# Hybrid decoder layer on one core: the order of ScalarE's sums and copies in the forgetting stage, and the sample's own key product in four pieces

## The chip, the core and the metric

The kernel runs on one core of a Trainium2 chip. The metric is the device time of one execution in microseconds. Three runs of the kernel before gave 3106.99, 3108.30 and 3108.68 us, a median of 3108.3.

The engines are called as in the profile: PE is TensorE, PEld its weight loads, DVE VectorE, ACT ScalarE, POOL GpSimd, SP SyncE (here only the queue from which DMAs are issued). Each engine runs its own instructions in order; they wait for one another through semaphores.

## The reference, cut to what matters

One decoder layer runs for a prompt of 2048 tokens and a sample group of 8 sequences with one new token each. It has three mixers: dilated windows, forgetting attention and a state-space scan, then a gated feed-forward. The change lies in forgetting attention alone (4 heads of 64):

```python
# prompt: every query against all earlier keys
s = einsum('bqhe,bkhe->bhqk', qb, k) * SCALE
s = s + cq[..., :, None] - cum[:, :, None, :]      # cum: running sum of the log forget rates
s = where(causal, s, NEG_INF)
o = einsum('bhqk,bkhe->bqhe', softmax(s, axis=-1), vf)

# sample: one query against 4096 paged past keys and its own key
s_past = einsum('bthe,bshe->bhts', q, past_k) * SCALE + suffix + cn
s_new  = einsum('bthe,bshe->bhts', q, k) * SCALE   # the sample's own key
p = softmax(concatenate([s_past, s_new], axis=-1), axis=-1)
```

## The kernel before

`fox_stage` does forgetting attention. The prompt is cut into 16 blocks: 4 heads of 4 blocks of 512 queries, with 4, 8, 12 and 16 key tiles of 128 (the order of the sizes is turned round for odd heads). A step over one key tile is a slot; there are 160. Every engine walks the same slots in its own program, and the order within a slot is written out by hand.

For a block each score is computed twice. First comes `score` (L1033): 128 queries by up to 512 keys, in one of three banks of `s_ps`. DVE takes its row maximum (`maximum`, L869, reduction at L880), and ACT's `exp_sum` (L963, instruction L967) turns it into exponentials in place and adds them up; an accumulator read belongs to it. These sums are the denominators. `score` number u waits until the sum of number u - 3 is done, since it uses the same bank. They run one block ahead: during block b the scores of block b + 1 are done, and `scores_at` says which at which slot (one or two, or none). Second comes `score_turned` (L1055, L1069 to L1072) of the running block, keys by queries, with the block's maximum already inside; ACT's `exp` (L955, L961) writes the probabilities, and `value` (L1075, L1089) multiplies four tiles of them by V.

A part is a piece of 512 tokens of queries, keys or rates that is brought into place for later blocks. PE transposes it into the bank `z_ps` (`part`, L1015, transposes at L1028 and L1030). ACT's `high` (L933) copies it rounded to fp32r: for queries L939 and L940, for keys L945 and L946, for rates L948 alone. DVE's `low` (L854; L861 for queries, L865 for keys) waits for that copy and writes the rest of the value, so that two matmuls together keep the precision. `parts_at` (L461 to L465) says at which slot: there are 30 in the loop, and 29 of them fall on a slot that also has one or two scores. The bank z is also used by `turn_max` (L1100, L1104: the block's maxima as rows; ACT copies them at L953) and `turn_o` (L1093, L1097: the block's output turned back, which DVE scales at L905 and SP stores at L623). Each use waits for the one before it (`z_wait`, L1001).

Beside this the sample's decode runs, spread over the same slots by `Beside`. SP loads the pages (L615, 256 KB each) into a ring of 11 groups of four, POOL multiplies keys by the query (L678), DVE reduces (L709), and then, for each half of a sample's pages (16 halves, nine slots apart): PE turns the maxima (L821), DVE's `spread` (L720) takes the top (L722, L723), PE hands it to all partitions (L824), DVE subtracts (`shifted`, L729 to L733), ACT takes exponentials (L791, L792), PE multiplies by the page values (L804) and DVE's `keep` (L751, L757 to L768) adds the result to `o_heads`. L821 of one half waits until `keep` of the half before has read the bank (L763).

The sample's own key is handled once, in the opening. POOL multiplies `q_all` by `k_own` (L668, 8 samples of 256 columns) after its loads have landed. At slot 5 (`SET_UP`) DVE, behind its low half of that slot, adds `logf` to `rest` (L697), reduces the product per head (L702), scales it (L703) and sets `setup_done`. At slot 6 SP waits for that before it loads pages into the part of the ring that `k_own` occupied.

Order in a slot. PE: decode steps, scores, turned score, value, part, turn_o. DVE: decode steps, maxima, denominators, low half, normalise. ACT: decode exponentials, copy of the output, exp, high copies of the part, sums.

Of the kernel before, what the change touches and what calls it, by code (L numbers as in the profile page):

```python
# [16 lines left out]
ALU = mybir.AluOpType  # L17
ACT = mybir.ActivationFunctionType
AX = mybir.AxisListType
# [5 lines left out]
DEC = 8  # L25
# [5 lines left out]
HD = 64  # L31
# [403 lines left out]
def fox_stage(nc, area, load_next, inputs, pa, consts_d, gates, mb, kv_d, logf_s_d, logf_stored):  # L435
# [12 lines left out]
    GROUP, PROBS = 4, 6  # L448
    first_group = [f // GROUP for f in first]
    tiles_in = [[(j, k) for k in range(q + 1) for j in range(4)] for _, q in blocks]  # L450

    scores_at = {}
# [40 lines left out]
    def part_slot(a, step):  # L493
        return 5 + 9 * a + step

    with ExitStack() as ctx:
        def sb(name, shape, dt=F32):
            return ctx.enter_context(nc.sbuf_tensor(f"fp_{name}", shape, dt))
# [4 lines left out]
        def sem(name):  # L503
            return ctx.enter_context(nc.semaphore(f"fp_{name}"))
# [26 lines left out]
        s_own = sb("s_own", [P, DEC, H])  # L531
# [12 lines left out]
        k_own = spare[:, 4096:6144].rearrange("p (b f) -> p b f", b=DEC)  # L544
        q_all = spare[:, 6144:8192].rearrange("p (b f) -> p b f", b=DEC)
# [28 lines left out]
        own_mult, setup_done = sem("own_mult"), sem("setup_done")  # L574
# [6 lines left out]
        dve = Steps(sem("dve"))  # L581
# [3 lines left out]
        def quarter(n):  # L585
            at = n % RING
            ring, at = (kv_low, at) if at < RING - 4 else (kv_high, at - (RING - 4))
            return ring[:, at * QUART:(at + 1) * QUART]
# [76 lines left out]
        def decode_pool(pool):  # L665
            yield 2
            pool.wait_ge(own_landed, 16 * (4 + COLS))
            pool.tensor_tensor(k_own, q_all, k_own, ALU.mult).then_inc(own_mult, 1)  # L668

            def product(a, k):  # L670
                n = a * QUARTS + k
                pool.wait_ge(page_landed[n % RING], 16 * QUART * (n // RING + 1))
                if a % 2 == 0 and k == 0:
                    pool.wait_ge(q_in[a // 2 % 2], 16 * (a // 4 + 1))
                if n >= 2:
                    pool.wait_ge(reduced, n - 1)
                for pair in (slice(0, 2), slice(2, 4)):
                    last = pool.tensor_tensor(prod[:, n % 2, pair], quarter(n)[:, pair, 0],  # L678
                                              q_own[:, a // 2 % 2:a // 2 % 2 + 1].to_broadcast([P, 2, F]), ALU.mult)
                last.then_inc(multiplied, 1)  # L680

            for slot in range(part_slot(0, 0), part_slot(PARTS, 0)):
                yield slot
                for a in range(PARTS):
                    at = slot - part_slot(a, 0)
                    if at in range(0, 2 * QUARTS, 2):
                        product(a, at // 2)

        def decode_vector(v):
# [8 lines left out]
                                        rest[:].rearrange("p b h g -> p (b h) g"),  # L698
                                        logf[:].rearrange("p b h -> p (b h)").unsqueeze(2)
                                        .to_broadcast([P, DEC * H, PAGES]), ALU.add))  # L700
            v.wait_ge(own_mult, 1)
            dve.link(v, v.reduce_sum(s_own[:], k_own.rearrange("p b (h e) -> p b h e", e=HD), AX.X))  # L702
            dve.link(v, v.tensor_scalar(s_own[:], s_own[:], SCALE, None, ALU.mult))  # L703
            v.sem_inc(setup_done, 1)

# [144 lines left out]
        @block.vector  # L850
        def _(v):
            beside = Beside(decode_vector(v))

            def low(kind, *at):  # L854
# [75 lines left out]
        @block.scalar  # L930
        def _(act):
            beside = Beside(decode_scalar(act))

            def high(kind, *at):
                act.wait_ge(part_turned, part_no[kind, *at])
                z = z_ps
                if kind == "q":
                    r = at[0] % 3
                    act.activation(q_both[0:HD, r], z[0:HD], ACT.Copy, scale=SCALE)  # L939
                    last = act.activation(q_more[HD:P, r], z[0:HD], ACT.Copy, scale=SCALE)  # L940
                else:
                    x, cs = (at[0] % 2, slice(at[1] * QB, (at[1] + 1) * QB)) if kind == "k" else (
                        0, slice(at[0] * QB, (at[0] + 1) * QB))
                    if kind == "k":
                        act.activation(k_both[x][0:HD, cs], z[0:HD], ACT.Copy)  # L945
                        last = act.activation(k_both[x][HD:P, cs], z[0:HD], ACT.Copy)  # L946
                    else:
                        last = act.activation(k_more[x][0:AUGS, cs], z[0:AUGS], ACT.Copy)  # L948
                last.then_inc(part_hi, 1)

            def shift(b):
                act.wait_ge(m_turned, b + 1)
                act.activation(q_more[0:AUGS, b % 3], z_ps[0:AUGS], ACT.Copy).then_inc(m_rows, 1)  # L953

            def exp(b, i):  # L955
                u, q = first[b] + i, blocks[b][1]
                w = QB - max(0, i - 4 * q) * P
                act.wait_ge(turned, u + 1)
                if u >= PROBS:
                    act.wait_ge(valued, (u - PROBS) // GROUP + 1)  # L960
                act.activation(probs[:, u % PROBS, 0:w], t_ps[:, u % 2, 0:w], ACT.Exp).then_inc(exped, 1)  # L961

            def exp_sum(b, n):  # L963
                q, (j, k), u = blocks[b][1], tiles_in[b][n], first[b] + n
                s = s_ps[:, u % 3, 0:QB if k < q else (j + 1) * P]
                act.wait_ge(maxed, u + 1)
                act.activation(s, s, ACT.Exp, bias=neg[:, b % 2, j, k:k + 1],  # L967
                               accum_out=den[:, b % 2, j, k:k + 1]).then_inc(summed, 1)

            def exp_scale(b):  # L970
                at = scale[:, b % 2, :, 0:blocks[b][1] + 1]
                act.wait_ge(scale_in, b + 1)
                act.activation(at, at, ACT.Exp).then_inc(scale_ready, 1)

            def copy_o(b):
                act.wait_ge(valued, first_group[b + 1])
                if b:
                    act.wait_ge(o_turned, b)
                act.activation(oT[:], o_ps[:], ACT.Copy).then_inc(o_copied, 1)

            for b, (h, q) in enumerate(blocks):
                for i in range(size[b]):
                    beside.until(first[b] + i)
                    if i == 0 and b > 0:
                        copy_o(b - 1)
                    exp(b, i)
                    for part in parts_at.get((b, i), []):
                        high(*part)
                    for n in scores_at.get((b, i), []):
                        exp_sum(b + 1, n)  # L990
                if b + 1 < NBLK:
                    shift(b + 1)
                    exp_scale(b + 1)
            copy_o(NBLK - 1)
            beside.until(SLOTS + 100)
# [2855 lines left out]
```

## Time and profile before

| | us |
|---|---|
| median of 3 runs | 3108.3 |
| profiled execution | 3103.8 |
| its span | 3101.8 |
| granted clock, mean over the span | 0.976 |

| engine | busy in the span (3101.8 us) | busy in the forgetting stage (628 to 1018 us) |
|---|---|---|
| PE | 2931.8 | 328.4 |
| DVE | 1612.8 | 279.2 |
| ACT | 966.8 | 232.8 |
| POOL | 758.9 | 177.7 |

The profile's rows of groups give a line, an engine, an operation, the tiles written and read, the count, and then busy time, mean length, and idle time before with what ended it. A row of the timeline gives the start and the length in microseconds, then engine, line, operation and tiles; in brackets stands how long the engine had been idle before it and what ended that idle time. Tiles of the forgetting stage are called `fp_...`; `fp_store` holds the split queries and the keys of even heads, `fp_k_both` and `fp_k_more` the keys of odd heads.

### The profile page before, as it was taken

To read this page: it belongs to the slowest core of one execution; us is meant where nothing else is said; L and a number is where in the kernel's file an instruction comes from. 1 tells how busy PE (TensorE), PEld (TensorE's weight loads), DVE (VectorE), ACT (ScalarE), POOL (GpSimd) and SP (SyncE) were. 2 spreads that over 40 slices of the span, in tenths; PEclk is the share of its full clock that TensorE was granted. 3 is DMA by queue.
4 is the path that set the end of the run, shared out by engine and by line. 5 is a ranking of instruction groups with operands and counts; after the bars stand their busy time and mean duration, and the time that the engine had idled before them with its cause. 6 is when DMAs were issued, how large, how long until landed. Compare 5 with 4: busy or idle time off the path is not lost. (4 is left out here: it accounts for less than half of the span.)

```text
span 3101.8 us, 44538 instructions
## 1 busy us (share of the span) xinstructions
PE 2931.8 (95%) x15777; PEld 2466.8 (80%) x15777; DVE 1612.8 (52%) x3068; ACT 966.8 (31%) x2010; POOL 758.9 (24%) x570
## 2 busy tenths in 40 slices
PE   8999999978889899879979999999999999999998
PEld 5888889945445799768779999999997788888886
DVE  5122321257777688757655554455557444444445
ACT  4222322256566455533331211222213111111112
POOL 4001200035445354422202211112222111122210
PEclk9999999989999999989989999999999999999999
DMA  4554443476865343367551111111113411111101
GB/s 140 187 211 164 135 138 113 140 210 201 225 189 179 120 126 96 74 196 222 205 205 41 41 41 53 70 41 41 41 55 123 150 41 41 41 50 59 54 14 56
DMA packets 238390, 350.85 MB, mean 113 GB/s; under 512 B 75449, under 2 KB 173274, under 8 KB 232271
## 3 DMA queue, kind: packets, MB, share of 16 engines
q1 hardware_dynamic: 237303, 326.45, 33.6%
q0 software_dynamic: 944, 22.61, 2.0%
q8 instruction: 75, 1.23, 0.2%
q14 instruction: 68, 0.56, 0.1%
HBM read 284.19 MB, written 93.97 MB: 122 GB/s over the span
## 5 line engine op out<-in xcount | busy, mean ns | idle before, releaser
L2862 POOL TENSOR_TENSOR cm_dn_lo<-cm_dn_raw,cm_dn_hi 128x1024 fp32r<-128x1024 f32 x44 | 108.3, 2483 | 974.3 <-ACT cm_dn_hi L2911 974.3
L3152 PE MATMUL cm_g_ps<-cm_h_hi,cm_up_hi 128*128 128x344 f32 (+1 forms) x880 | 310.4, 353 | 11.1 <-DVE cm_h_lo L2967 10.9
L3154 PE MATMUL cm_g_ps<-cm_h_hi,cm_up_lo 128*128 128x344 f32 (+1 forms) x880 | 308.8, 351 | 0.0
L3152 PE MATMUL cm_u_ps<-cm_h_hi,cm_up_hi 128*128 128x344 f32 (+1 forms) x880 | 308.2, 350 | 0.0
L3153 PE MATMUL cm_g_ps<-cm_h_lo,cm_up_hi 128*128 128x344 f32 (+1 forms) x880 | 308.1, 350 | 0.0
L3154 PE MATMUL cm_u_ps<-cm_h_hi,cm_up_lo 128*128 128x344 f32 (+1 forms) x880 | 307.8, 350 | 0.0
L3153 PE MATMUL cm_u_ps<-cm_h_lo,cm_up_hi 128*128 128x344 f32 (+1 forms) x880 | 307.0, 349 | 0.0
L2855 POOL TENSOR_TENSOR cm_up_lo<-area,cm_up_hi 128x2048 fp32r<-128x2048 f32 x42 | 195.4, 4654 | 176.7 <-ACT cm_up_hi L2887 176.7
L2990 DVE TENSOR_SCALAR area<-area 128x344 f32<-128x344 f32 (+2 forms) x110 | 54.2, 493 | 330.4 <-ACT area L2904 189.6
L2900 ACT ACTIVATE area<-cm_g_ps 128x344 f32<-128x344 f32 (+1 forms) x110 | 55.0, 511 | 510.1 <-PE cm_g_ps L3154 509.9
L3152 PEld LDWEIGHTS cm_g_ps<-cm_h_hi,cm_up_hi 128*128 128x128 f32 x880 | 166.2, 189 | 36.3 <-issue 21.2
L3439 ACT ACTIVATE area<-pj_acc,area 128x480 f32<-128x480 f32 (+7 forms) x119 | 76.2, 641 | 345.8 <-PE pj_acc L3661 268.4
L3154 PEld LDWEIGHTS cm_g_ps<-cm_h_hi,cm_up_lo 128*128 128x128 f32 x880 | 166.4, 189 | 15.8
L3153 PEld LDWEIGHTS cm_g_ps<-cm_h_lo,cm_up_hi 128*128 128x128 f32 x880 | 166.3, 189 | 15.9
L3154 PEld LDWEIGHTS cm_u_ps<-cm_h_hi,cm_up_lo 128*128 128x128 f32 x880 | 165.4, 188 | 16.0
L3153 PEld LDWEIGHTS cm_u_ps<-cm_h_lo,cm_up_hi 128*128 128x128 f32 x880 | 165.3, 188 | 15.9
L3152 PEld LDWEIGHTS cm_u_ps<-cm_h_hi,cm_up_hi 128*128 128x128 f32 x880 | 165.2, 188 | 15.3
L3046 DVE TENSOR_TENSOR cm_y<-cm_y,cm_y_ps 128x1024 f32<-128x1024 f32 x88 | 107.4, 1221 | 122.8 <-PE cm_y_ps L3193 122.8
L2887 ACT ACTIVATE cm_up_hi<-area 128x2048 fp32r<-128x2048 f32 x44 | 84.3, 1917 | 278.6 <-PE cm_u_ps L3154 272.4
L3659 PE MATMUL pj_acc<-fp_store,pj_h_hi 128*128 128x480 f32 (+3 forms) x448 | 169.2, 378 | 0.9 <-DVE pj_h_lo L3508 0.9
L3660 PE MATMUL pj_acc<-fp_store,pj_h_hi 128*128 128x480 f32 (+3 forms) x448 | 167.8, 375 | 0.0
L3661 PE MATMUL pj_acc<-fp_store,pj_h_lo 128*128 128x480 f32 (+3 forms) x448 | 167.7, 374 | 0.0
(518 smaller groups left out, 7092.8 us busy)
## 6 DMA issues: line engine op xcount, KB each, us to landing
area<-in_w_up SPq DMA_DIRECT2D x44, 1024.0 KB, 7.0
fp_kv_low<-in_fox_kv SPq DMA_DIRECT2D x168, 256.0 KB, 3.0
area<-in_fox_kv SPq DMA_DIRECT2D x88, 256.0 KB, 2.9
cm_dn_raw<-in_w_down SPq DMA_DIRECT2D x44, 512.0 KB, 3.7
out_s_win<-in_cache POOLq DMA_DIRECT2D x8, 2047.0 KB, 8.3
area<-in_w_a SPq DMA_DIRECT2D x12, 960.0 KB, 7.9
proj_a<-area SPq DMA_DIRECT2D x48, 240.0 KB
sp_raw<-proj_b SPq DMA_DIRECT2D x16, 640.0 KB, 4.0
```

Source lines behind the costliest of these rows:

```text
L2855: pool.tensor_tensor(up_lo[:, s], up_raw[:, s], up_hi[:, s].bitcast(F32), ALU.subtract).then_inc(up_ready, 1)
L2862: pool.tensor_tensor(dn_lo[:, s], dn_raw[:, s], dn_hi[:, s].bitcast(F32), ALU.subtract).then_inc(dn_ready, 1)
L2887: act.activation(up_hi[:, s], up_raw[:, s], ACT.Copy).then_inc(up_hi_ready, 1)
L2900: act.activation(gate[:, s, HALO + at[b]:HALO + at[b + 1]], g_ps[:, b, 0:H.widths[b]], ACT.Copy).then_inc(gate_ready, 1)
L3046: v.tensor_tensor(y[:, n], y[:, n], sums(H, n).rearrange("p a n -> p (a n)"), ALU.add).then_inc(added, 1)
L3152: pe.matmul(out, hi, h_hi[:, k, cs], start=(k == 0), stop=False)
L3153: pe.matmul(out, hi, h_lo[:, k, cs], start=False, stop=False)
L3154: last = pe.matmul(out, lo, h_hi[:, k, cs], start=False, stop=(k == KT - 1))
L3439: act.activation(row[0:m, n % ROWS, 0:wide], acc[0:m, n % BANKS, 0:wide], ACT.Copy, scale=rstd[0:m, t:t + 1]).then_inc(evac, 1)
L3659: pe.matmul(out, h_hi[:, k, place(t)], w_hi[j % 2][:, k, 0:wide], start=(k == 0), stop=False)
L3660: pe.matmul(out, h_hi[:, k, place(t)], w_lo[j % 2][:, k, 0:wide], start=False, stop=False)
L3661: last = pe.matmul(out, h_lo[:, k, place(t)], w_hi[j % 2][:, k, 0:wide], start=False, stop=(k == KT - 1))
```

## The change

In `decode_pool` the one product over 8 samples becomes four over 2 samples each, each with its own step of `own_mult`. In `decode_vector` the one reduction over 8 samples becomes four, each waiting for its piece of the product. In ScalarE's loop over the slots, the loop over the slot's sums (`exp_sum`) and that over its parts (`high`) change places.

```diff
@@ decode_pool
             pool.wait_ge(own_landed, 16 * (4 + COLS))
-            pool.tensor_tensor(k_own, q_all, k_own, ALU.mult).then_inc(own_mult, 1)
+            for pair in range(0, DEC, 2):
+                two = slice(pair, pair + 2)
+                pool.tensor_tensor(k_own[:, two], q_all[:, two], k_own[:, two], ALU.mult).then_inc(own_mult, 1)
@@ decode_vector
-            v.wait_ge(own_mult, 1)
-            dve.link(v, v.reduce_sum(s_own[:], k_own.rearrange("p b (h e) -> p b h e", e=HD), AX.X))
+            for pair in range(0, DEC, 2):
+                two = slice(pair, pair + 2)
+                v.wait_ge(own_mult, pair // 2 + 1)
+                dve.link(v, v.reduce_sum(s_own[:, two], k_own[:, two].rearrange("p b (h e) -> p b h e", e=HD), AX.X))
             dve.link(v, v.tensor_scalar(s_own[:], s_own[:], SCALE, None, ALU.mult))
@@ scalar, the loop over a block's slots
                     exp(b, i)
+                    for n in scores_at.get((b, i), []):
+                        exp_sum(b + 1, n)
                     for part in parts_at.get((b, i), []):
                         high(*part)
-                    for n in scores_at.get((b, i), []):
-                        exp_sum(b + 1, n)
```

## Rows read from the trace of the kernel before

**Rows 1.** The page: busy time, share of the span and instructions of each engine.
```profile
PE 2931.8 (95%) x15777; PEld 2466.8 (80%) x15777; DVE 1612.8 (52%) x3068; ACT 966.8 (31%) x2010; POOL 758.9 (24%) x570
```

**Rows 2.** Table of stretches: stretch, length, busy time by engine, clock, DMA share, GB/s.
```profile
628.00:1018.00 390.00, 328.37 (x1968) 193.94 (x1968) 279.22 (x582) 232.79 (x608) 177.69 (x145) 0.93 0.69 199
```

**Rows 3.** Waits, 628 to 1018 us: who waited for whom, total, times, longest.
```profile
ACT fp_s L967 <- DVE fp_neg L880: 56.3, 46, 4.8
...
PE fp_s L1049 <- ACT fp_s L967: 21.1, 22, 2.5
...
DVE fp_k_more L865 <- ACT fp_k_both L946: 17.4, 7, 5.4
```

**Rows 4.** Lines L821 (first two rows) and L824: what ended their engine's idle time.
```profile
  DVE fp_o_heads L763: 9.3, 6
  DVE fp_o_part L763: 7.0, 6
...
  DVE fp_diag L723: 12.1, 11
```

**Rows 5.** Single lines: count, then shortest/median/longest in ns, first and last start.
```profile
L967 ACT ACTIVATE fp_s<-fp_s,fp_neg x156: 319/654/668, 631.7 to 1005.2; 128x512 f32<-128x512 f32 x111, 128x128 f32<-128x128 f32 x15, 128x256 f32<-128x256 f32 x15, 128x384 f32<-128x384 f32 x15
L967 ACT ACTIVATION_READ_ACCUMULATOR fp_s<-fp_s,fp_neg x156: 185/202/217, 632.2 to 1005.7; 128x1 f32 x156
...
L709 DVE TENSOR_REDUCE fp_s_dec<-fp_prod x64: 1201/1212/1223, 657.8 to 997.0; 128x16 f32<-128x1024 f32 x64
...
L678 POOL TENSOR_TENSOR fp_prod<-fp_kv_low,fp_q_own x84: 1254/1276/1459, 644.7 to 984.3; 128x512 f32<-128x512 f32 x84
```

**Rows 6.** Timelines of the opening: SP's queue, POOL, DVE and PE, 628 to 700 us.
```profile
634.52 31.06 SPq L615 DMA_DIRECT2D fp_kv_low<-in_fox_kv  x28
...
669.02 18.23 SPq L615 DMA_DIRECT2D area<-in_fox_kv  x16
687.29 0.43 SPq L623 DMA_DIRECT2D mix_b<-fp_o_tok  x1
...
639.00 4.52 POOL L668 TENSOR_TENSOR area<-area 128x2048 f32<-128x2048 f32 x1 [9.01 <-DMA fp_logf<-out_s_logf]
...
642.08 1.48 DVE L886 CAST fp_m_tok<-fp_top 128x4 fp32r<-128x4 f32 x1
...
653.02 2.29 DVE L702 TENSOR_REDUCE fp_s_own<-area 128x32 f32<-128x2048 f32 x1
...
690.48 0.42 DVE L905 TENSOR_TENSOR fp_o_tok<-fp_z,fp_rden 128x256 f32<-128x256 f32 x1 [5.68 <-DMA mix_b<-fp_o_tok]
...
693.19 1.03 PE L1030 MATMUL fp_z<-sp_consts,fp_k_tok 128*64 128x128 f32 x4 [3.83 <-DMA fp_k_tok<-proj_a]
```

**Rows 7.** Timelines of DVE and PE around slot 41.
```profile
751.07 0.68 DVE L880 TENSOR_REDUCE fp_neg<-fp_s 128x1 f32<-128x512 f32 x1
...
752.54 0.68 DVE L861 SCALAR_TENSOR_TENSOR fp_store<-fp_z,fp_store 64x512 fp32r<-64x512 f32 x1
...
753.83 0.27 PE L821 MATMUL fp_e<-sp_consts,fp_top_dec 128*4 128x128 f32 x1 [2.35 <-DVE fp_o_heads L763]
```

**Rows 8.** Timelines of ACT and PE around slot 105.
```profile
916.62 0.66 ACT L967 ACTIVATE fp_s<-fp_s,fp_neg 128x512 f32<-128x512 f32 x1 [0.64 <-DVE fp_neg L880]
...
917.86 1.10 PE L1097 MATMUL fp_z<-fp_fold,fp_oT 128*128 128x64 f32 x8 [0.68 <-DVE fp_store L861]
```

**Rows 9.** Timelines of DVE and PE behind slot 85.
```profile
858.85 0.68 DVE L861 SCALAR_TENSOR_TENSOR fp_store<-fp_z,fp_store 64x512 fp32r<-64x512 f32 x1 [0.95 <-ACT fp_store L940]
...
859.56 0.50 PE L1049 MATMUL fp_s<-fp_store 128*128 128x512 f32 x1 [1.62 <-ACT fp_s L967]
...
864.32 0.27 PE L821 MATMUL fp_e<-sp_consts,fp_top_dec 128*4 128x128 f32 x1 [1.83 <-DVE fp_o_part L763]
```

**Rows 10.** Timelines of ACT and PE around slot 97.
```profile
894.97 0.59 ACT L945 ACTIVATE fp_k_both<-fp_z 64x512 fp32r<-64x512 f32 x1 [1.83 <-PE fp_z L1030]
...
896.98 0.50 PE L1049 MATMUL fp_s<-fp_store 128*128 128x512 f32 x1 [1.58 <-ACT fp_s L967]
```

## The prediction

> **What bounds the kernel now.** I read five views in this order. The page's busy shares name TensorE (95%) [rows 1], but a share over the span says nothing of one stage, and the edit touches only the forgetting stage. Its window, 628 to 1018 us, is next [rows 2]: PE is busy 328 of 390 us, DVE 279, ACT 233. So PE has some 62 us of holes there, and anything that opens or closes a hole on PE moves the end, since every later stage starts after this one.
>
> The waits of the stage [rows 3] name two sorts of hole. The first is what the edit aims at: a prompt score (L1049) waits for ACT's sum (L967) of the tile three scores earlier, 21.1 us seen on PE. The same waits show ACT's sum waiting 56.3 us for DVE's maximum, so ACT isn't simply late; DVE often is. Third, DVE itself stands 17.4 us in front of the low half of a key part (L865) until ACT's high copy (L946) is done. DVE runs in order, so whatever stands behind that low half stands too.
>
> The second sort of hole is at the sample's decode steps [rows 4]: PE waits for DVE at L821 (until `keep` has read the output bank, 9.3 + 7.0 us in 12 times) and at L824 (until `spread`, 12.1 us in 11 times). These 28.4 us say that DVE is the later of the two engines at nearly every decode step. This decides the case: what makes DVE's low half later makes the next L821 or L824 later, and PE with it.
>
> **Part 1, ScalarE's order.** At 29 of the 160 slots there is both a part and a score to sum (12 slots with two sums, 17 with one). Before, ACT does: exp, high copies, sum(s). After: exp, sum(s), high copies. No instruction is added. PE and DVE keep their order: PE does scores, turned score, value, part transposes; DVE does maxima, then the low half. A sum costs 0.66 + 0.20 for its accumulator read [rows 5], less about 0.1 in which the two overlap: 0.75 us. The two copies cost 1.2 us (0.59 each, as the first of them in [rows 10]).
>
> So a sum ends up to 1.2 us earlier and the copies start up to 0.75 us (one sum) or 1.5 us (two) later. Queued behind the late copy: on ACT the next slot's exp; on DVE the low half, and behind it the reductions of the sample's products, the decode steps and the next maxima; on PE the next user of bank z (turn_o, turn_max or the next part). The part is free of delay only where the sums fit into time in which ACT waits for PE's transposes anyway. I walked the slots in the timeline, giving each engine its order and the durations it has there:
>
> Opening, slots 0 to 13. Earlier sums gain 0.7 us of PE at slot 0 and 1.3 us by slot 2; the late low half of slot 3 leaves 0.4 of that. Slot 5 (two sums) makes DVE 1.5 us later, slot 13 again 1.5. With 0.4 us of part 2 that is 1.5 + 1.5 + 0.4 - 0.4 = 3.0 us late at 687 us. None of this reaches the end, because a chain with no arithmetic in it ends last here [rows 6]: SyncE issues 28 page loads without a gap from 634.52 on, 16 more from 669.02, only then the store of the first output (687.29) and the next keys. DVE's L905 waits 5.68 us for that store, and PE's first part of head 1 waits 3.83 us for the keys. Neither the gate on the setup (L644, reached at about 668 us, opened at 655.5) nor those loads hang on the moved work. 3.0 is under 3.83: the opening costs nothing, with 0.8 us to spare.
>
> From 693 us on nothing covers. The slots, by kind:
> - Parts that come after a `value` (slots 29, 61, 73, 89): ACT waits 1 to 3 us for the transposes with the maxima long there, so the sums go into that wait. Copy and low half stay where they were, and the next waits of PE are on DVE: 0.
> - Slots 17 to 21: the same at first, PE gets its score 1.0 us earlier, and later copies give it back: -0.2.
> - One sum, maximum ready, copy late by one sum (slots 25, 63, 121, 137): L824, turn_max and L821 follow directly or through instructions without a gap. 0.8 + 0.75 + 0.75 + 0.8 = 3.1.
> - One sum whose maximum isn't ready, so that the copies wait for the maximum too. Slot 41 [rows 7]: the maximum ends at 751.75, the sum takes until 752.5, the copies until 753.7, so the low half starts at 753.75 instead of 752.54; behind it L763, and L821 on PE, which already waited 2.35 us for it: +1.2. Slot 105 [rows 8]: the sum starts at 916.62 as before, its 0.75 and the copies' 1.2 last until 918.57, the low half (0.68 [rows 7]) until 919.3, and turn_o, which had waited 0.68 us for it and started at 917.86, starts at about 919.35: +1.5. By the same working slots 57, 69 and 77 give 0.7 each (there DVE had other work before the low half). Together 1.2 + 1.5 + 2.1 = 4.8.
> - Two sums: slot 85 [rows 9]. The score after it waited 1.62 us for its sum and now doesn't; but the low half, which waited 0.95 us for the copy, moves 1.5 us, and so do the reductions and L763 behind it; at L821 PE had to wait 1.83 us and now waits for what it gained and 1.5 more: +1.5. Slot 81 is alike, with some 0.8 us covered by a store that L905 waits for at 850.49 (a second wait of the kind of L905 in [rows 6]): +0.7. Slot 93: DVE had 1.0 us of rest behind it: +0.5. Together 2.7.
> - Slots 97 to 101 [rows 10]: the sums of 97 fit into the 1.83 us before the copy, the score behind gains 1.58; then copy and low half of slot 99 are 0.55 late, those of 101 1.45, and turn_max 1.1. +1.1.
>
> Sum: 0 - 0.2 + 3.1 + 4.8 + 2.7 + 1.1 = 11.5 us. Three terms (63, 93 and 97 to 101, 2.35 us) I read through more than one wait, where part can be lost in others' slack; I count them at half: **+10.3 us**.
>
> **Part 2, the product in four pieces.** POOL's 4.52 us [rows 6] become four of the size of a page product, 1.28 us each [rows 5]: 5.1 us, ending at 644.1, before the first page product starts (644.71, which waited for its DMA). On DVE one reduction of 2048 columns takes 2.29 [rows 6] and one of 1024 takes 1.21 [rows 5], so 1.05 ns a column and 0.14 us fixed: four of 512 take 2.7 us, +0.4; three more links to itself cost between 0 and 0.1 us each. Nothing is gained by overlap: DVE comes to it at 653.0, POOL was done at 643.5. All four waits are met. Both additions lie in the opening, under the same loads: 0. If the cover is gone, it is 0.4 to 0.7 us. One side effect in the cover: the cast L886 at 642.08 [rows 6] took 1.48 us and ended with POOL's product; pieces could let it go earlier by up to 1.4 us. I take 0 for the whole, with +0.7 and nothing below it for the range, as 690.48 is set by the store.
>
> The Trainium skill (Perfetto Trace Analysis, Optimizing Scalar/DVE Operations) says that where these engines aren't saturated but cause bubbles elsewhere, breaking up instructions may let work complete sooner. By that rule both parts would pay; the trace agrees on the bubbles but not, for the pieces, on work that could start sooner. What it would give is rival A.
>
> **Rivals.**
> A, faster: the freed sums are what PE gets. The score waits right after the changed slots from 693 us on are 0.37, 0.72, 1.79, 1.62, 1.58 and 0.71 us, six of one pattern of which 1.62 and 1.58 stand in [rows 9, 10]: 6.8 us. If the late low halves are taken up by DVE's rests, the end is 6.8 us earlier. Place: DVE between the low half and the next L821 or L824; it decides where DVE rests there for longer than the copy is late (0.75 to 1.5 us). For it: 21.1 us of such waits. Against it: [rows 4]. 3101.5.
> B, no change: only the delays handed over directly count (25, 41, 69, 77, 105: 0.8 + 1.2 + 0.7 + 0.7 + 1.5 = 4.9), the others drown, or half of A comes off the forecast (10.3 - 6.8 = 3.5). 3111.8 to 3113.2.
> C, slower still: the cover of the opening fails, because the pieces or slot 13 cost over 0.8 us more than I think; up to 3.0 comes on top of 11.5: 3122.8.
> D, the order isn't what matters (ACT stands at the maximum whichever way): 0, part of B.
>
> **How the numbers follow.** The profiled execution took 3103.8 us (span 3101.8), 4.5 under the median of 3108.3. The working gives 3103.8 + 10.3 = 3114.1 for such an execution, and on the scale of the median 3108.3 + 10.3 = 3118.6. A measurement of this kernel can tell about 0.2% (6.2 us) from no change. Chances: forecast 0.57, C 0.11, B with D 0.20, A 0.12. The range takes in the forecast, B and most of C and leaves out A and the far end: 3104 to 3124. Slower 0.68, within 0.2% 0.20, faster 0.12.
>
> **What would show it.** Right: L967's releases of L1049 fall by 5 us or more after 693 us, while PE's waits for DVE at L821, L824, L1097 and L1104 and DVE's wait for L940/L946 grow by more; the low half of slot 41 starts 1.2 us later after its maximum; L905 still waits for a store and L1030 for the keys near 690 us, each about 3 us less; the stage ends 10 us later and later stages keep their length. Wrong: PE's waits at L821 and L824 don't grow (A), or head 1's first part no longer waits for a DMA (C).

## The result and the profile after

The changed kernel took 3126.9 us (median of 6 runs) against 3106.2 us before (6 runs): a ratio of 1.0069, 95% interval [1.0053, 1.0086], so 16 to 27 us slower. The forecast was slower by 10.3 us, 3118.6, with 3104 to 3124 as its range. The direction was right, the size was half of what came.

| | before | after |
|---|---|---|
| profiled execution, us | 3103.8 | 3119.8 |
| span, us | 3101.8 | 3117.8 |
| granted clock over the span | 0.976 | 0.973 |
| forgetting stage, first POOL memset to last normalise, us | 389.9 | 409.1 |
| DVE's idle time in front of the low halves (L861 and L865; after L865 and L869), us | 38.4 | 54.5 |

Lines after are 4 higher from `decode_vector` on: L971 is the sum, L944 and L950 are the second copies, L865 and L869 the low halves, L767 is in `keep`, L825 and L828 are PE's decode steps, L1053 is the score, L1101 is turn_o.

The stage as a whole, from the table of stretches of the kernel after (stretch, length, busy time by engine, clock, DMA share, GB/s), answers [rows 2]:

```profile
628.00:1037.00 409.00, 336.61 (x1968) 199.31 (x1968) 278.75 (x585) 233.70 (x608) 177.14 (x148) 0.91 0.67 189
```

The engines' work is what it was (DVE 278.8 for 279.2, ACT 233.7 for 232.8), the stage is 19 us longer, and PE's busy time is 8 us longer for the same matmuls, at a mean clock of 0.91 where it was 0.93. What follows the stage keeps its length: from its end to the end of the span it is 2081.2 us after and 2083.8 before, and between 2082 and 2087 in three other traces that have the old order of ScalarE from slot 14 on (`e2`, `e4` and `e7` below). The waits of the stage after, which answer [rows 3] and [rows 4]:

```profile
ACT fp_s L971 <- DVE fp_neg L884: 73.5, 53, 5.6
...
PE fp_s L1053 <- ACT fp_s L971: 20.1, 18, 4.9
DVE fp_k_more L869 <- ACT fp_k_both L950: 17.7, 7, 3.6
...
PE fp_e L825 <- DVE fp_o_heads L767: 11.6, 6, 3.6
...
PE fp_e L825 <- DVE fp_o_part L767: 9.6, 6, 3.6
...
PE fp_z L1101 <- DVE fp_store L865: 7.5, 7, 2.1
```

PE's wait for ACT's sums, at which the edit aims, fell by 1 us (21.1 to 20.1). From 693 us on it fell from 10.9 to 9.0, where the prediction had named 5 us or more as a sign of being right. PE's waits for `keep` went from 16.3 to 21.2 and those of turn_o from 2.4 to 7.5. ACT's sums wait 17 us longer for DVE's maxima than before (56.3). At L828 (L824 before) the view of the single line has 15.1 us where it had 12.1:

```profile
  DVE fp_diag L727: 15.1, 11
```

Why so little of that wait went away is seen behind slot 81, which has two sums and a part. At slot 82 PE's wait for a sum fell from 1.79 to 0.56 us, at slot 86 from 1.62 to 0.45, at slot 98 from 1.58 to nothing. But at slot 83 it grew from 0.96 to 3.45 us. After, from the timelines of DVE, ACT and PE:

```profile
854.05 0.69 DVE L865 SCALAR_TENSOR_TENSOR fp_store<-fp_z,fp_store 64x512 fp32r<-64x512 f32 x1 [2.25 <-ACT fp_store L944]
...
856.31 1.07 DVE L884 TENSOR_REDUCE fp_neg<-fp_s 128x1 f32<-128x128 f32 x3
...
856.62 0.34 ACT L971 ACTIVATE fp_s<-fp_s,fp_neg 128x128 f32<-128x128 f32 x1 [2.27 <-DVE fp_neg L884]
...
857.13 0.80 PE L1053 MATMUL fp_s<-fp_store 128*128 128x512 f32 x1 [3.45 <-ACT fp_s L971]
```

The low half waited 2.25 us for the late copy (0.98 before), the maxima stand behind it on DVE, the next sum waits for the maxima and the score for the sum. So the new order makes a later sum late.

Slot 41 after, from the timelines of ACT, DVE and PE, answers [rows 7]:

```profile
753.11 0.66 ACT L971 ACTIVATE fp_s<-fp_s,fp_neg 128x512 f32<-128x512 f32 x1 [0.82 <-DVE fp_neg L884]
...
755.07 0.68 DVE L865 SCALAR_TENSOR_TENSOR fp_store<-fp_z,fp_store 64x512 fp32r<-64x512 f32 x1 [1.24 <-ACT fp_store L944]
755.78 0.42 DVE L767 TENSOR_TENSOR fp_o_heads<-fp_e,fp_mask 128x256 f32<-128x256 f32 x1
...
756.35 0.27 PE L825 MATMUL fp_e<-sp_consts,fp_top_dec 128*4 128x128 f32 x1 [3.57 <-DVE fp_o_heads L767]
756.38 0.48 PE L1053 MATMUL fp_s<-fp_k_both,fp_store 128*128 128x512 f32 x1
...
758.42 0.77 PE L1053 MATMUL fp_s<-fp_k_both,fp_store 128*128 128x512 f32 x1
...
762.93 2.84 PE L1093 MATMUL fp_o<-fp_probs,fp_v_tok 128*64 128x512 f32 x8
```

The slot comes 1.3 us later than before, so the low half (752.54 before) is 1.2 us later in its slot and so is L825 (753.83 before), whose wait grew from 2.35 to 3.57 us. That is the forecast's term (1.2 us). Then comes what it had not: a score that took 0.48 us at 756.38 takes 0.77 at 758.42, and the eight value matmuls 2.84 us where they took 1.94. The stretches around it, in the kernel after:

```profile
751.00:756.40 5.40, 1.83 (x12) 1.19 (x10) 3.96 (x10) 3.73 (x9) 2.49 (x2) 1.00 0.75 243
756.40:772.00 15.60, 15.60 (x84) 8.94 (x86) 10.43 (x20) 8.81 (x23) 7.53 (x6) 0.78 0.70 193
```

and in the kernel before:

```profile
755.00:771.00 16.00, 15.78 (x100) 8.68 (x99) 14.19 (x27) 9.65 (x28) 10.30 (x8) 1.00 0.75 224
```

PE is busy without a gap after and all but 0.2 us before, but behind the longer hole it runs part of the time at 1.2 instead of 2.4 GHz (a mean of 0.78 of full clock).

The opening after, from the timelines of POOL, DVE, SP and PE, answers [rows 6]:

```profile
638.34 4.96 POOL L670 TENSOR_TENSOR area<-area 128x512 f32<-128x512 f32 x4 [8.98 <-DMA fp_logf<-out_s_logf]
...
639.41 0.21 DVE L890 CAST fp_m_tok<-fp_top 128x4 fp32r<-128x4 f32 x1
...
652.18 2.85 DVE L706 TENSOR_REDUCE fp_s_own<-area 128x8 f32<-128x512 f32 x4
...
686.81 0.43 SPq L623 DMA_DIRECT2D mix_b<-fp_o_tok  x1
...
690.26 0.42 DVE L909 TENSOR_TENSOR fp_o_tok<-fp_z,fp_rden 128x256 f32<-128x256 f32 x1 [2.35 <-DMA mix_b<-fp_o_tok]
```

The four products take 4.96 us (5.1 forecast), the four reductions 2.85 (2.7 to 3.0 forecast), and the store of the first output is issued and lands within half a microsecond of where it did. The cast takes 0.21 us instead of 1.48, but the instruction behind it (L891, L887 before) now takes 1.19 us instead of 0.17, so the two together gain 0.25 us. DVE has 2.35 us of cover left of 5.68, 3.3 us less where 3.0 were forecast. Part of that agreement is luck, because the first trace of before is the one with the most cover: the others with the old order in the opening have 3.73 (the same kernel again, `e7`), 3.72 (`e2`, with the pieces) and 4.08 (`e3`) left, those with the new order 2.35, 2.47 (`e4`) and 1.79 (`e1`). Means of 4.3 and 2.2 us put the cost of the new order in the opening at some 2 us.

### The profile page after: what moved, and what is told of

The parts are those of the page before. It is cut to its first block and busy times, and to the rows that moved or that the text cites. A ratio compares the mean times of both kernels' runs of the same rounds, so it can differ in the third digit from the quotient of the medians.

```text
span 3117.8 us, 44547 instructions
## 1 busy us (share of the span) xinstructions
PE 2939.0 (94%) x15777; PEld 2471.7 (79%) x15777; DVE 1613.3 (52%) x3071; ACT 967.8 (31%) x2010; POOL 757.5 (24%) x573
## 5 line engine op out<-in xcount | busy, mean ns | idle before, releaser
L3156 PE MATMUL cm_g_ps<-cm_h_hi,cm_up_hi 128*128 128x344 f32 (+1 forms) x880 | 310.0, 352 | 11.1 <-DVE cm_h_lo L2971 10.9
L3156 PEld LDWEIGHTS cm_g_ps<-cm_h_hi,cm_up_hi 128*128 128x128 f32 x880 | 165.9, 188 | 36.4 <-issue 21.3
```

Of the source, the lines that this page charges most:

```text
L3156: pe.matmul(out, hi, h_hi[:, k, cs], start=(k == 0), stop=False)
```

## The experiments

**One part at a time.** Two kernels carry one half of the change each.

`e1_sums_only` is the kernel before with, in ScalarE's loop:

```diff
+                    for n in scores_at.get((b, i), []):
+                        exp_sum(b + 1, n)
                     for part in parts_at.get((b, i), []):
                         high(*part)
-                    for n in scores_at.get((b, i), []):
-                        exp_sum(b + 1, n)
```

> The whole change without the four pieces: the sums stand ahead of the copies at all 29 slots, the sample's own key product is one instruction. Theory (the late low half, and the clock that falls behind PE's longer holes): all of the loss comes from the order, so this runs 1.005 to 1.008 of the kernel before, and the forgetting stage ends 16 to 20 us later. Rival (the four pieces and their links cost part of it): at or under 1.004.

Measured: 1.0053 [1.0038, 1.0068] (3123.6 us against 3106.7). Its stage ends 21.8 us later than in the first trace of before, more than the 16 to 20 expected, and 12 to 18 us later than in the other three traces with the old order from slot 14 on. `e2_pieces_only` has the two other hunks of the change and ScalarE's order as before:

```diff
-            pool.tensor_tensor(k_own, q_all, k_own, ALU.mult).then_inc(own_mult, 1)
+            for pair in range(0, DEC, 2):
+                two = slice(pair, pair + 2)
+                pool.tensor_tensor(k_own[:, two], q_all[:, two], k_own[:, two], ALU.mult).then_inc(own_mult, 1)
...
+            for pair in range(0, DEC, 2):
+                two = slice(pair, pair + 2)
+                v.wait_ge(own_mult, pair // 2 + 1)
```

> The four pieces alone, with ScalarE's order as before. Theory: 0, since all of it lies under SyncE's chain of page loads up to 690 us; 1.000 within 0.001, and the store that DVE's normalise waits for lands at the same time. Rival (pieces cost): 1.002 or more, with PE's first part of head 1 later than 693 us.

Measured: 1.0000 [0.9989, 1.0011]. The loss is that of the order; the pieces cost nothing that can be measured, which here means under some 3.5 us.

**The opening alone.** `e4_opening_only` has the pieces, and the new order at slots 0 to 13 only:

```diff
+                    sums_first = first[b] + i <= 13
+                    if sums_first:
+                        for n in scores_at.get((b, i), []):
+                            exp_sum(b + 1, n)
                     for part in parts_at.get((b, i), []):
                         high(*part)
-                    for n in scores_at.get((b, i), []):
-                        exp_sum(b + 1, n)
+                    if not sums_first:
+                        for n in scores_at.get((b, i), []):
+                            exp_sum(b + 1, n)
```

> Four pieces, and the sums ahead of the copies at slots 0 to 13 only. Theory: up to 4 us late inside the opening, 0 from slot 18 on, because PE still waits for the keys' load at about 693 us; 1.000 within 0.001. Rival (the opening isn't covered): 1 to 4 us more at slot 24, 1.001.

Measured: 1.0005 [0.9984, 1.0025]. In its trace the turned score of slot 17 starts 4.8 us later than in the first trace of before, that of slot 24 0.6 us later. So the opening is covered but for 0.6 us, which is within what two traces of one kernel differ by; the interval of the time alone would allow 8 us. The reason in the expectation held only in part: PE's first part of head 1 starts at 695.05 us here, without a wait for the keys.

**One slot alone.** `e3_slot41_only` has the same edit on the kernel before, with `sums_first = first[b] + i == 41`.

> The sum stands ahead of the copies at slot 41 alone. Theory: the low half starts 1.2 us later, L821 behind it 1.2 us later; then TensorE's granted clock falls for some 15 us and the shift grows to 3 to 5 us by slot 52, so 1.001 to 1.0015. Rival without the clock (late handovers alone): the shift stays at 1.2 us, and the growth seen in the changed kernel between slots 43 and 52 came from elsewhere.

Measured: 1.0007 [0.9993, 1.0022], too wide to tell anything by itself. The trace tells it. Two rows of DVE's and PE's timelines, then two stretches:

```profile
752.22 0.68 DVE L861 SCALAR_TENSOR_TENSOR fp_store<-fp_z,fp_store 64x512 fp32r<-64x512 f32 x1 [1.24 <-ACT fp_store L940]
...
753.50 0.27 PE L821 MATMUL fp_e<-sp_consts,fp_top_dec 128*4 128x128 f32 x1 [3.55 <-DVE fp_o_heads L763]
```

```profile
755.60:772.00 16.40, 16.40 (x86) 8.75 (x85) 11.04 (x22) 8.24 (x22) 10.06 (x8) 0.82 0.62 192
772.00:790.00 18.00, 15.33 (x103) 8.83 (x102) 16.02 (x33) 11.29 (x31) 9.88 (x9) 1.00 0.87 233
```

Against the trace of before, the shift of the turned score is -1.5 us at slots 32 to 42, -0.3 at slot 43 (the 1.2 us of the late low half) and +3.2 at slot 52. One slot's new order makes slots 41 to 53 take 26.0 us, as in the changed kernel, where the kernel before takes 21.3 (before and a second trace of it, and `e4`; in `e2`, also with the old order there, it is 22.8, with the same wait of 2.35 us and a clock of 0.93), and the clock behind it is 0.82 where it was 1.00. Part of it comes back: by slot 62 the shift is 1.6, because low stretches that the kernel before has around slots 61 to 69 are shorter here (18.7 against 20.0 us).

**Is it the clock?** If the long hole at L821 lowers the clock, then filling it with matmuls should bring the growth back to 1.2 us. `e5_before_filled` and `e6_after_filled` are before and after with eight dummy matmuls ahead of L821 at the slots that have a score; they write the bank that the next score overwrites:

```diff
+            def fill_wait(slot, count):
+                b = next(b for b in range(NBLK) if slot < first[b + 1])
+                scores = scores_at.get((b, slot - first[b]), [])
+                if not scores:
+                    return
+                u = first[b + 1] + scores[0]
+                pe.wait_ge(summed, u - 2)
+                for _ in range(count):
+                    pe.matmul(s_ps[:, u % 3, 0:QB], q_both[:, b % 3, 0:P], k_both[blocks[b][0] % 2][:, 0:QB],
+                              start=True, stop=True)
...
                     if at == 11:
+                        fill_wait(slot, 8)
                         pe.wait_ge(rest_ready, 1)
```

> The kernel before, with eight dummy 512-column matmuls (about 1.8 us at full clock) on PE ahead of L821 at the slots that have a score; they write the score bank that the next score overwrites. They should lie in the wait for DVE's keep where that is about 2 us, and cost up to 1.8 us where it is short. Theory: by itself between 3 us faster (less time at the low clock) and 10 us slower. It is there for the difference to its twin.

> The changed kernel with the same dummy matmuls ahead of L821. Theory with the clock: PE has no long hole there any more, so the clock stays up behind L821, and the difference to its twin without the change is near the 11.5 us of late handovers, less what the dummies would have cost in short waits, 7 to 13 us. Rival (the rest of the 20 us is no matter of the clock): the difference stays at 17 to 21 us.

Measured: 1.0015 [1.0001, 1.0028] and 1.0069 [1.0053, 1.0086] of the kernel before, so the difference stayed at 17 to 19 us. By the number that I had written down the rival had it. The traces say why it's no such clear verdict. Slots 41 to 53, where the filling reaches, take 22.8 us in the one and 24.0 in the other: 1.2 us apart, the late low half and nothing else, and the clock behind the filled hole is full in the changed kernel too:

```profile
766.00:782.00 16.00, 16.00 (x97) 9.06 (x96) 13.83 (x25) 9.63 (x27) 10.31 (x8) 1.00 0.76 237
```

But slot 79, where the wait at L821 grew from 2.18 to 2.86 us, has no score and so no dummies, L824 had none anywhere, and in the opening the dummies of slot 16 used up the cover: `e6` is 10 us late at slot 16 and keeps 4.1 more than its twin at slot 24.

So the filling was done again, from slot 24 on, six matmuls ahead of each L821 and each L824, with or without a score in the slot: `e10_before_all_filled` and `e11_after_all_filled`.

```diff
                     if at == 11:
+                        fill_wait(slot, 6)
...
                     if at == 13:
+                        fill_wait(slot, 6)
```

> The kernel before with six dummy matmuls (1.4 us) ahead of each L821 and each L824 from slot 24 on, whether the slot has a score or not. Here for the difference to its twin: 5 to 20 us slower than the kernel before, since many of the 28 places have no wait to hide them.

> The changed kernel with the same dummies. Theory (late handovers as worked out, and the rest the clock): between slots 77 and 81 the twins differ by under 1.5 us where the unfilled kernels differ by 2.5 to 3.4, between 24 and 29 by under 2 us instead of 2.5 to 3.4, and the sum behind slot 24 is 9 to 13 us instead of 16 to 20. Rival (the excess is late handovers that I missed): the segments differ as without the dummies, sum 16 us or more.

Measured: 1.0019 [1.0005, 1.0033] and 1.0078 [1.005, 1.0106]. Slots 77 to 81 in the kernel after and in `e11`, from the tables of stretches:

```profile
836.00:850.40 14.40, 11.16 (x54) 7.71 (x54) 8.84 (x23) 7.59 (x22) 5.55 (x5) 0.76 0.77 230
```

```profile
840.60:853.40 12.80, 11.19 (x67) 8.00 (x67) 8.47 (x23) 7.72 (x22) 5.62 (x5) 1.00 0.75 239
```

With 13 matmuls more the stretch is 1.6 us shorter, at full clock instead of 0.76. The table below is worked out from the starts of the turned score's first matmul (L1069 before) at the two slots, in every trace; "old order" are two traces of before, `e2` and `e4`, "new order" are after and `e1`.

| slots | old order | new order | filled, old and new (`e10`, `e11`) | forecast of the difference |
|---|---|---|---|---|
| 24 to 29 | 9.2 to 12.0 | 12.6, 12.9 | 9.8, 10.4 | 0.8 |
| 29 to 41 | 26.7 to 27.0 | 26.6, 26.7 | 29.2, 29.9 | 0 |
| 41 to 53 | 21.3 to 22.8 | 26.0, 28.5 | 23.7, 26.5 | 1.2 |
| 57 to 61 | 9.4 to 9.8 | 10.2, 10.5 | 9.2, 9.9 | 0.7 |
| 61 to 69 | 19.8 to 21.9 | 19.2, 22.0 | 18.7, 19.2 | 0.75 |
| 69 to 77 | 20.7 to 20.8 | 22.7, 20.9 | 20.6, 22.6 | 0.7 |
| 77 to 81 | 11.1 to 14.0 | 14.5, 14.5 | 12.1, 12.8 | 0.7 |
| 81 to 85 | 16.9 to 18.6 | 18.0, 18.1 | 16.4, 17.7 | 0.7 |
| 85 to 93 | 24.5 to 27.7 | 25.9, 25.9 | 24.0, 26.7 | 1.5 |
| 93 to 97 | 9.6 | 9.9, 9.9 | 10.4, 10.8 | 0.5 |
| 97 to 105 | 20.8 to 20.9 | 21.6, 21.6 | 21.2, 21.6 | 1.1 |
| 105 to 121 | 32.9 | 34.7, 34.6 | 36.2, 39.5 | 1.5 |
| 121 to 137 | 29.3 to 31.9 | 32.2, 32.2 | 33.2, 33.8 | 0.75 |
| 137 to the end | 43.1 | 43.8, 43.8 | 45.6, 46.2 | 0.8 |

Where the clock is full or nearly so in all of them (93 to 121, 137 on) old and new order differ by 0.4, 0.7, 1.8 and 0.7 us, against 0.5, 1.1, 1.5 and 0.8 forecast. Where they differ by more than the forecast (24, 41, 77, 121) the new order has the lower clock, and filled at full clock the difference falls to 0.6 at 24, 0.6 at 77 and 0.7 at 121. At 41 and 105 `e11` has low stretches again and differs by 2.8 and 3.3.

Slots 53 to 57 (7.0 us, 8.6 in the filled pair) are the same in both orders and left out.

From slot 24 to the end: the four old-order traces take 306.0, 310.0, 315.9 and 309.9 us, the new-order ones 325.0 and 329.1, so 16.6 us more on the mean. The time at 1.2 GHz in it (twice the share of the clock that is missing, by segment) is 24, 38, 55 and 27 us against 45 and 55, 13.8 more on the mean. The two old-order traces that are furthest apart in clock give a price: (315.9 - 306.0) / (54.6 - 23.7) = 0.32 us for each us at the low clock. So 4.4 of the 16.6 us would be the clock and 12.2 late handovers. The filled pairs give by the same price 17.3 - 4.2 = 13.1 and 17.7 - 5.5 = 12.2. The price is rough. It differs by place: at slots 97 to 105 the clock was 0.92 in two old-order traces and 1.00 in the other two, and all four took 20.8 to 20.9 us, while at slots 41 to 53 `e2` took 1.5 us more for 3.2 us at the low clock. And not only the clock differs between the traces: `e4` is 3.9 us longer than the first trace with 3.6 us more at the low clock, 1.7 us of it at slots 81 to 85, where its clock is the higher one (0.91 against 0.80).

A second estimate does without the price: for each stretch (slots 69 to 77 and 85 to 93 in two halves each), take the old-order traces whose clock there is nearest to that of the new-order trace. Outside slots 41 to 53, where no old-order trace has so low a clock, the differences add up to 9.5 us for the kernel after and 10.8 for `e1`; the forecast for these stretches was 10.5. With the 1.2 us of slot 41 that makes 10.7 to 12.0 us of late handovers and leaves 4.6 to 5.9 of the 16.6 to the clock. Both splits are estimates; slot 41 with and without filling is what is shown. This pair too broke the number that I had set for it (9 to 13 us in all, 17.3 measured), because the filled kernel with the new order still spent 20 us at the low clock, its twin 7.

**A second trace of before.** `e7_before_again` is the kernel before, unchanged.

> The kernel before once more, for a second trace: how far two traces of one program differ in the stage. Both theories: slots within 1 us of the first trace up to 750 us, and the clock of each stretch within 0.05.

Measured: 3111.7 us, its stage 394.7 us where the first trace had 389.9. The two differ by more than I expected: up to 1.7 us in the opening, 1.3 to 1.6 us (the second one ahead) at slots 28 to 40, 2.5 us (the second one behind) by slot 92, and slots 124 to 126 add 1.5 at a lower clock. The first trace, on which the forecast was built, was the one with the least time at the low clock of the four with the old order.

**Is it DVE's decode steps behind the low half?** If so, letting the low half stand in the next slot, behind that slot's decode steps, should take the loss away although ScalarE keeps its new order. `e8_before_low_later` and `e9_after_low_later` are before and after with, on DVE:

```diff
+            slots = [(b, i) for b in range(NBLK) for i in range(size[b])]
             for b in range(NBLK):
                 for i in range(size[b]):
                     if first[b] + i > SET_UP:
                         beside.until(first[b] + i)
+                    for part in parts_at.get(slots[first[b] + i - 1], []) if b + i else []:
+                        low(*part)
                     for n in scores_at.get((b, i), []):
                         maximum(b + 1, n)
                     if i == 1:
                         denominators(b)
-                    for part in parts_at.get((b, i), []):
-                        low(*part)
```

> The kernel before with one edit on DVE: the low half of a slot's part stands in the next slot, behind that slot's decode steps, so that keep, spread and the reductions no longer stand behind a low half that waits for ScalarE. Theory (what costs is DVE's decode steps behind the low half): 0 to 10 us faster than the kernel before, 0.997 to 1.000. Rival (the order of the low half is no matter): 1.000.

> The changed kernel with the same edit on DVE. Theory: the late copies now hold back nothing that decode needs, so the loss shrinks from 20 us to under 7 against its twin with ScalarE's old order, and 0.998 to 1.003 of the kernel before. Rival (the loss comes from ScalarE's own queue, the exps that stand behind the late copies, or from somewhere else): the difference to the twin stays at 14 us or more.

Measured: 0.9974 [0.9961, 0.9988] and 0.9974 [0.9961, 0.9987]. The 17 to 21 us between the two orders of ScalarE are gone, and both are some 8 us faster than the kernel before; for the second that is a little more than its range allowed. Slot 41 in `e9`, from the timelines of DVE and PE:

```profile
749.20 0.42 DVE L767 TENSOR_TENSOR fp_o_heads<-fp_e,fp_mask 128x256 f32<-128x256 f32 x1
...
749.76 0.27 PE L825 MATMUL fp_e<-sp_consts,fp_top_dec 128*4 128x128 f32 x1 [1.63 <-DVE fp_o_heads L767]
...
750.40 0.68 DVE L865 SCALAR_TENSOR_TENSOR fp_store<-fp_z,fp_store 64x512 fp32r<-64x512 f32 x1 [0.78 <-ACT fp_store L945]
```

`keep` now runs ahead of the low half, and L825 waits 1.63 us (3.57 after, 2.35 before). The low half still waits for ScalarE's copy, but the decode steps no longer stand behind it.

Slot 41 also shows what this doesn't settle. Slots 41 to 53 in `e8` and in `e9`, from the tables of stretches:

```profile
746.68:767.25 20.57, 18.73 (x114) 10.76 (x113) 18.92 (x37) 13.86 (x36) 12.80 (x10) 1.00 0.75 227
```

```profile
746.13:770.64 24.51, 22.03 (x114) 12.44 (x113) 18.16 (x38) 14.62 (x37) 12.57 (x10) 0.86 0.82 235
```

PE waits 1.64 us for `keep` in the one and 1.63 in the other, yet the clock stays up in `e8` and falls in `e9`, which is 3.9 us longer there and not slower as a whole. At slot 88 it is the other way round: the wait there grew from 1.83 us before to 3.61 after, and the mean clock in the 16 us behind it was 0.79 before and 0.90 after. So the length of this one wait doesn't by itself decide what the clock does behind it; what else does stays open.

**A version that beats both.** `e12_low_later_scores_first` is `e9` with, on PE, a slot's scores ahead of its decode steps:

```diff
                 for i in range(size[b]):
-                    beside.until(first[b] + i)
                     for n in scores_at.get((b, i), []):
                         score(b + 1, n)
+                    beside.until(first[b] + i)
```

> The changed kernel with the low half in the next slot, and on PE a slot's scores ahead of its decode steps instead of behind them, so that a score can run where PE waits for keep or spread. Theory: the waits at L821 and L824 that are left shrink by up to 0.5 us each, 0 to 8 us faster than the same kernel without it (0.995 to 0.998 of the kernel before). Rival: decode steps come later by a score, DVE's spread and shifted wait for them, and it is 0.998 to 1.001.

Measured: 0.9947 [0.9926, 0.9968], 3096.4 us against 3111.6 of before in the same runs. The interval overlaps that of `e9` (0.9961 to 0.9987), so what the scores add to the moved low half isn't shown by the times alone. Of its waits in the stage:

```profile
PE fp_e L825 <- DVE fp_o_heads L767: 2.3, 2, 1.9
...
PE fp_z L1102 <- DVE fp_store L865: 13.6, 10, 5.0
```

With 0.4 us at the other form of L767, PE waits 2.7 us for `keep` where it waited 16.3 before and 21.2 in the changed kernel. What is left on PE is 15.2 us for ACT's sums, turn_o behind the low half, 13.6 us, and 8.8 us for the keys of head 1 in the opening, which is no longer hidden.

## Why the prediction was right and wrong

**The direction and its reason held.** The forecast said that the freed sums are worth nothing where DVE is the later engine, and that each late copy reaches PE through the low half and the decode steps behind it. `e1` puts the loss on the order (1.0053 against 1.0069, with intervals that overlap), slot 41 shows the chain and its 1.2 us, and `e8` with `e9` take the loss away by unhooking the decode steps from the low half.

**The opening and the pieces held.** 0 forecast, `e2` 1.0000, `e4` 1.0005. The cover was 5.68 us on DVE in the first trace of before, 3.7 to 4.1 in three others with the old order there, and is 2.35 after. One sign went against me: I had written that PE's first part of head 1 would still wait for its keys, about 3 us less, and that without this wait rival C would be true. It starts at 694.47 in the trace after, 1.3 us later than before and without a wait for the DMA. Yet slot 18 starts 0.9 us earlier than before, so nothing was added behind it. The cover was used up nearly whole; `e6`, with more in the opening, spilled 4 us.

**The step that failed: a sum of late handovers alone.** The sum had 11.5 us and was cut to 10.3. Late handovers come to some 11 to 13 us by the estimates above, so the 11.5 were about right. Of the three terms counted at half, two can be read: slots 93 and 97 gave 0.4 and 0.7 of 0.5 and 1.1, more than half and less than the whole. Others gave more than their term (slots 81 to 85 1.1 to 1.2 for 0.7, slots 105 to 121 1.8 for 1.5), so cutting the sum by 1.2 us made it worse. What the sum lacked was a term for TensorE's clock. I had its mean in front of me (0.93 in [rows 2]) and the length of each hole in the bracket of each row, and priced a hole of 3.6 us at the 1.2 us by which it was longer. Behind it the mean clock over some 16 us was 0.78 (0.82 in `e3`, 0.62 in `e1`), which made it 4.7 us in slots 41 to 53. Over the stage it comes to some 4 to 6 us by the estimates above. That the clock fell behind the longer wait at slot 41 is shown there three times (after, `e1`, `e3`), and filling the wait undid it; but `e9` and slot 88 show that the length of such a wait doesn't foretell it, so the term couldn't have been worked out from the length alone.

**A step that was wrong and cost little in the sum: the freed sums.** The working let the waits for sums go at slots 85 and 97, and they did (1.62 to 0.45 us, 1.58 to 0). It named the next maxima among what stands behind the late low half, but priced nothing for them. They make a later sum late: at slot 83 this gave 3.45 us of wait for 0.96, and with slot 82's gain of 1.23 it makes the 1.1 to 1.2 us that slots 81 to 85 lost, for which 0.7 was forecast by another path. That is why the sign of 5 us didn't come (1.9 us).

**A term outside the sum.** The forecast rested on one trace of before, the one with the shortest stage of four. Others with the same order of ScalarE, `e4` from slot 14 on, are 394.7, 395.0 and 399.4 us long instead of 389.9. That made neither the direction nor the handovers wrong, but a few microseconds either way were never in reach of a single trace.

**Rival A** (faster by 6.8) fell: PE's waits behind the changed slots did shrink in three places, but the stretches of slots they lie in (81 to 85, 85 to 93, 97 to 105) are no shorter than in the first trace of before. The rule that breaking up instructions may let work complete sooner (the Trainium skill, Perfetto Trace Analysis, Optimizing Scalar/DVE Operations) speaks of ScalarE's and VectorE's instructions. Changing the order breaks up none, so the prediction was wrong to say that by this rule both parts would pay; and the reduction that was broken up started no sooner by it, since its product was long done.

**What stays open.** The medians differ by 20.7 us, the stages from slot 24 on by 16.6 on the mean of six traces. The interval (16.5 to 26.7) holds both, so I can't say whether there is anything more than scatter between them. The filled pairs differ by 17 to 19 us in their medians and 17.3 and 17.7 in the stage, as the rivals to the clock had it; they don't bear out the clock as more than the smaller part of the loss. Why the clock falls behind some waits and not behind others of the same length is open. Nor is it settled how far the differences of 2.8 and 3.3 us at slots 41 and 105 in the filled pair are clock, since both have low stretches.

## What to carry to other kernels

Before moving a step ahead of another on one engine, look at who stands behind the step that becomes late: here ScalarE's copy released an in-order VectorE instruction, behind which all of the decode work stood, and that cost more than the freed sum gave. The cure was to move the waiting instruction behind the work that doesn't need it, not to change who is served first. And don't price a hole on TensorE by its length alone: look at the granted clock in the stretch behind it, and take a second trace of the same kernel before believing a few microseconds.

## What the runs showed of the hardware

A hole on PE that grew from 2.35 to 3.57 us (3.55 in `e3`) was followed by 16 us at a mean of 0.78 (0.82) of full clock, where before it was 1.00, though PE was busy without a gap in those 16 us; with eight dummy matmuls in the hole the clock stayed at 1.00. But 16 us behind a wait of 1.63 us had a mean of 0.79 in `e9` and 1.00 behind one of 1.64 in `e8`, and at slot 88 it was 0.90 behind a wait of 3.61 us and 0.79 behind one of 1.83. Kernels with the same order of work differ in this by themselves: 24 to 55 us at the low level from slot 24 on in four traces, and up to 10 us of stage time with it.

Filling holes with dummy matmuls raised the clock (from slot 24 on, 7 us at the low level in `e10`, 24 in the first trace of before), but cost 0.15 to 0.2% in time: it is a means to measure, not to gain. And a VectorE cast of 4 columns took 1.48, 2.67, 2.67 and 3.22 us in four traces, and ended each time with GpSimd's product of 4.5 us beside it; with the product in four pieces it took 0.21 to 0.40 us in three, but the 4-column instruction behind it then took 1.2 us where it had taken 0.17.
